# One decoder step on one core: attention passes written out unit by unit, with two score buffers per head, 64-row score tiles and 64-column values

## What is computed

```
s = einsum('nbqhgd,nbkhd->nbhgqk', qb, k2) * SCALE + bias      # 128 queries by 256 keys, head size 64
m = max(s, -1);  e = exp(s - m);  den = sum(e, -1)
o = einsum('nbhgqk,nbkhd->nbqhgd', e / den, v2)
lse = m + log(den)                                            # used to weigh head groups or the sink
```

## Time and profile before

| | before |
|---|---|
| median of 3 runs | 3253.78 us (3252.25 to 3257.07) |
| profiled execution, its own time | 3262.15 us |
| its span in the profile | 3260.3 us |
| mean granted TensorE clock | 0.939 of full speed |
| PE busy | 2920.5 us, 90% of the span |
| DVE, ACT, POOL busy | 1284.9, 894.0, 817.0 us |

### The profile page before, as it was taken

How to read it: one execution, slowest core, us unless ns; L and a number is a source line. 1 busy time by engine, 2 the same in 40 slices (tenths; PEclk the granted TensorE clock), 3 DMA queues, 4 the chain that set the end, 5 groups by cost and what they waited for, 6 DMA issues and landing times. The chain is left out here.

```text
span 3260.3 us, 54005 instructions
## 1 busy us (share of the span) xinstructions
PE 2920.5 (90%) x20802; PEld 2648.9 (81%) x20802; DVE 1284.9 (39%) x1934; ACT 894.0 (27%) x1725; POOL 817.0 (25%) x834
## 2 busy tenths in 40 slices
PE   8999989646899999999999999989945887899998
PEld 7999988525899998999989898979832224899997
DVE  2222243575422224222243434443368774422223
ACT  2222123431322212222222423242334331322212
POOL 2221112162122211222102123112326652122210
PEclk9999999957999999999999999999966888999999
DMA  7776622002466563666523142314216775466651
GB/s 245 247 234 168 206 60 70 5 24 64 144 221 211 162 205 126 220 212 209 181 63 93 38 121 67 91 32 123 73 41 223 272 272 190 141 211 223 214 167 44
DMA packets 467039, 482.09 MB, mean 148 GB/s; under 512 B 61054, under 2 KB 440047, under 8 KB 462632
## 3 DMA queue, kind: packets, MB, share of 16 engines
q1 hardware_dynamic: 456880, 467.46, 43.9%
q0 software_dynamic: 6416, 12.20, 1.3%
q10 hardware_dynamic: 3616, 0.69, 0.1%
HBM read 466.46 MB, written 199.42 MB: 204 GB/s over the span
## 5 line engine op out<-in xcount | busy, mean ns | idle before, releaser
L779 PE MATMUL bank<-sb_xh,sb_wl 128*128 128x272 f32 x4416 | 957.6, 293 | 50.7 <-DVE sb_wl L1483 28.5
L783 PE MATMUL bank<-sb_xh,sb_wh 128*128 128x272 f32 x4416 | 945.0, 291 | 0.0
L781 PE MATMUL bank<-sb_xl,sb_wh 128*128 128x272 f32 x4416 | 942.1, 290 | 0.0
L1483 DVE TENSOR_TENSOR sb_wl<-sb_raw,sb_wh 128x1024 fp32r<-128x1024 f32 (+1 forms) x340 | 453.0, 1333 | 1001.7 <-ACT sb_wh L1219 992.8
L779 PEld LDWEIGHTS bank<-sb_xh,sb_wl 128*128 128x128 f32 x4416 | 711.9, 191 | 58.8 <-DVE sb_wl L1483 31.9
L781 PEld LDWEIGHTS bank<-sb_xl,sb_wh 128*128 128x128 f32 x4416 | 712.8, 191 | 0.7
L783 PEld LDWEIGHTS bank<-sb_xh,sb_wh 128*128 128x128 f32 x4416 | 707.8, 191 | 0.0
L1219 ACT CAST sb_wh<-sb_raw 128x1024 fp32r<-128x1024 f32 (+1 forms) x340 | 376.4, 1109 | 972.7 <-PE bank L783 941.9
L1912 POOL CAST sb_hh<-sb_h 128x544 f32 x88 | 130.1, 1479 | 756.2 <-DVE sb_h L1492 756.2
L779 PE MATMUL bank<-sb_hh,sb_wl 128*128 128x272 f32 x1408 | 311.7, 292 | 0.5 <-DVE sb_wl L1483 0.5
L783 PE MATMUL bank<-sb_hh,sb_wh 128*128 128x272 f32 x1408 | 304.4, 288 | 0.0
(11 more groups left out here) (244 smaller groups left out, 2749.6 us busy)
## 6 DMA issues: line engine op xcount, KB each, us to landing
out_state_b_s<-in_cache_b_kv SPq DMA_DIRECT2D x176, 704.0 KB, 6.3
sb_dkvb<-in_cache_b_kv SPq DMA_DIRECT2D x144, 512.0 KB, 5.6
sb_raw<-in_ffn_w_gate SPq DMA_DIRECT2D x88, 512.0 KB, 3.9
sb_raw<-in_ffn_w_up SPq DMA_DIRECT2D x88, 512.0 KB, 4.5
sb_raw<-in_ffn_w_down SPq DMA_DIRECT2D x64, 704.0 KB, 4.8
sb_raw<-in_attn_b_w_qkv SPq DMA_DIRECT2D x72, 512.0 KB, 3.7
out_state_b_s<-in_cache_b_kv SPq DMA_DIRECT2D x32, 1016.0 KB, 8.1
out_state_b_s<-in_cache_b_kv SPq DMA_DIRECT2D x44, 176.0 KB
```

The lines of the kernel that those rows point to most:

```text
L779: pe.matmul(acc(s, h), wl[slot][:, k, :], hi(k)[:, halves[h]], start=start and k == 0, stop=False)
L781: pe.matmul(acc(s, h), wh[slot][:, k, :], lo(k)[:, halves[h]], start=False, stop=False)
L783: last = pe.matmul(acc(s, h), wh[slot][:, k, :], hi(k)[:, halves[h]], start=False, stop=end)
L1483: dve.tensor_tensor(wl[j % 2][:, 0:ph.chunks, :], raw[j][:, 0:ph.chunks, :], v.bitcast(F32), ALU.subtract).then_inc(wl_rdy, 1)
```

## The change

`skewed` now writes all units of a pass out, in the order in which the loop ran them; no registers are left in the passes. `scores` takes the queries straight from `q`: each head multiplies its own 64 partitions (`tile_position=(hd * HD, 0)`, a row tile), into its own bank (0 or 1 for the first head, 6 or 7 for the second). `values` takes only the head's own 64 columns. `add_bias` reads the two banks with two instructions and writes the maximum into `md`; `exps` reads it there and writes its sums there. `stats`, the staging on POOL, its clearing (`clear_staging`) and the tiles `qs`, `nm`, `dn` are gone. Those who waited for `st_done` wait for `ex_done`.

```
-        def skewed(eng, n_pairs, stages):
...
-            with eng.Fori(1, n_pairs) as i:
-                for s_ in range(4):
-                    for fn, lag in stages:
-                        fn(i + (s_ - lag) // 4, (s_ - lag) % 4)
+        def skewed(ps, stages):
+            for s_ in range(ps.units + max(lag for _, lag in stages)):
                 for fn, lag in stages:
+                    if 0 <= s_ - lag < ps.units:
+                        fn(s_ - lag, (s_ - lag) // 4, (s_ - lag) % 4)
...
-                    pe.wait_ge(qs_rdy, i * 4 + (ps.u0 + blk + 1))
-                    pe.wait_ge(sm_done, i * 4 + (ps.u0 + blk + 1))
+                def scores(k, i, blk):
+                    pe.wait_ge(sm_done, ps.u0 + k + 1)
                     for hd in range(2):
+                        rows = slice(hd * HD, (hd + 1) * HD)
...
+                            mm = pe.matmul(bank[6 * hd + k % 2][:, c:c + n], R["q"][g][rows, i, blk * P:(blk + 1) * P],
+                                           R["k"][g][rows, kt_, keys], start=True, stop=True, tile_position=(hd * HD, 0))
...
-                            mm = pe.matmul(bank[2 + b][:, hd * P:(hd + 1) * P], R["kt"][b][:, c:c + P], src,
+                            own = slice(vt * P + hd * HD, vt * P + (hd + 1) * HD)
...
+                            mm = pe.matmul(bank[2 + k % 2][:, hd * HD:(hd + 1) * HD], R["kt"][k % 2][:, c:c + P], src,
...
+                        last = act.activation(x, x, ACT.Exp, bias=md[:, blk, 0, c:c + 1], accum_out=md[:, blk, 1, c:c + 1])
...
-                    dve.scalar_tensor_tensor(x, s, SCALE, R["bias"][:, bass.ds(i * 2, 2), c0:256], ALU.mult, ALU.add).then_inc(sm_done, 1)
+                    for hd in range(2):
+                        last = dve.scalar_tensor_tensor(x[:, hd], bank[6 * hd + k % 2][:, c0:256], SCALE,
+                                                        R["bias"][:, 2 * i + hd, c0:256], ALU.mult, ALU.add)
...
-                skewed(dve, ps.pairs, [(add_bias, 0), (stats, 1), (output, 3)])
+                skewed(ps, [(add_bias, 0), (output, 3)])
...
-            def attention(ps, rn):
...
-                skewed(pool, ps.pairs, [(stage, 0)])
```

More of the change, by code:

```diff
@@ L988, in values @@
                         for kb in kbs:
[L989 to L992, removed]
+                            own = slice(vt * P + hd * HD, vt * P + (hd + 1) * HD)
+                            src = R["v"][kb][:, blk, own] if ps.dilated else R["v"][0][:, blk - 1 + kb, own]
                             c = hd * 256 + kb * P
-                            mm = pe.matmul(bank[2 + b][:, hd * P:(hd + 1) * P], R["kt"][b][:, c:c + P], src,
+                            mm = pe.matmul(bank[2 + k % 2][:, hd * HD:(hd + 1) * HD], R["kt"][k % 2][:, c:c + P], src,
                                            start=kb == kbs[0], stop=kb == kbs[-1])
                     mm.then_inc(pv_done, 1)
-                skewed(pe, ps.pairs, [(scores, 0), (turn, 1), (values, 2)])
+                skewed(ps, [(scores, 0), (turn, 1), (values, 2)])
                 end = ps.u0 + ps.units
@@ L1617, in output @@
[L1617 to L1628, removed]
@@ L1631, in step, with output @@
+                def output(k, i, blk):
+                    dve.wait_ge(pv_done, ps.u0 + k + 3)
+                    dve.tensor_copy(R["o"][ps.slot][:, blk, i * P:(i + 1) * P], bank[2 + k % 2][:, 0:P]).then_inc(oev_done, 1)
+                skewed(ps, [(add_bias, 0), (output, 3)])
             def step(ins):
@@ L1660, in group_weights @@
                 ps = pass_b[2 * r + 1]
-                dve.wait_ge(st_done, ps.u0 + ps.units)
+                dve.wait_ge(ex_done, ps.u0 + ps.units)
                 dve.wait_ge(oev_done, ps.u0 + ps.units + 2)
@@ L1855, in _ @@
                         dve.wait_ge(sink_rdy, 1)
-                        dve.wait_ge(st_done, pass_a.units)
+                        dve.wait_ge(ex_done, pass_a.units)
                         dve.wait_ge(oev_done, pass_a.units + 2)
@@ L1955, in run @@
                 store_out(r, r.n - 1)
[L1957 to L1964, removed]
-            def attention(ps, rn):
[L1967 to L1976, removed]
-                            last = pool.tensor_copy(R["qs"][b][rows, 2 * g + hd, :], src)
-                    last.then_inc(qs_rdy, 1)
-                skewed(pool, ps.pairs, [(stage, 0)])
             def exchange(ps):
                 r = (ps.n - 1) // 2
-                pool.wait_ge(st_done, ps.u0 + ps.units)
+                pool.wait_ge(ex_done, ps.u0 + ps.units)
                 pat = "(u c) e -> u c e" if ps.dilated else "(c u) e -> u c e"
@@ L2043, in _ @@
                     n_norm += 1
-                    if ph.kind == "down" and ph.f == 0:
-                        clear_staging(ph.l)
                     if ph.next:
@@ L2050, in _ @@
                     if ph is qkv[0]:
-                        attention(pass_a, ph.run)
                         decode(0)
@@ L2054, in _ @@
                         r, y = ph.run.rnd, int(ph.run.items[0][1] > 0)
-                        attention(pass_b[2 * r + y], ph.run)
                         exchange(pass_b[2 * r + y])
```

85 lines of the change are left out of this document (33 added, 52 removed).

## The result

| | before | after |
|---|---|---|
| median of 16 runs each | 3256.98 us (3249.88 to 3261.75) | 3271.21 us (3257.85 to 3294.62) |
| profiled execution, its span | 3262.15, 3260.3 us | 3273.63, 3271.8 us |
| mean granted TensorE clock | 0.939 | 0.917 |

The ratio is 1.0045, with an interval of 1.0031 to 1.0058. The kernel became 0.45% slower; I had forecast 1% faster. The 16 runs also scatter over 37 us, where the 16 of before scatter over 12. They stand almost in the order of their granted clocks: the fastest (3257.85 us) had 0.924, the slowest (3294.62 us) 0.907.

A forecast was written before the change was run, and what follows sets the result against it. The attention passes were taken as bound by a loop through PE and the other engines' answers. Loops -12.3 and -6.4, starts -12.0 sum to -30.7 us: 3231.5 profiled, 3223 as a median; range 3205 to 3257.

The forecast's parts named there:

- rival C: In the passes, PE is less busy and the clock falls to 1.2 GHz: +13.4 us, 3267 us; chance 0.12.
- Scores as row tiles: In the score products, both heads' row tiles run fully in parallel, so scores fall from 1.03 to 0.61 us.
- Rival A: In the scores, the two heads' row tiles don't overlap: loops lose 20.5 us, median 3244 us; chance 0.14.
- Changing between tile sizes: Between values and scores on PE, each change costs 0.20 us; one per loop charged, bounds 0 and 0.40.
- Rival D: Tile-size changes cost twice as much, the one before the turn not hidden: +9.6 us, 3233 us; within the forecast's 0.55.
- Values of 64 columns: In the value passes, each still needs its 0.11 us weight load, so no gain; bounds 0 or 0.055 us per pass.
- Rival B: 64-column value passes do gain, 0.055 us each, if loads go faster: 17.6 us, 3205 us; chance 0.10.
- Register work: In the pass loops, delays before values (596.10 to 596.40) and before DVE's bias (0.23 us, elsewhere 0.03) go when written out.
- DVE: Bias in two instructions takes 0.79 us for 0.73, +0.06; the dropped copies of `stats` count nothing.
- Starts: At the start of four passes, scores begin 2.4, 2.4, 3.6 and 3.6 us earlier: -12.0 us.
- The loops together: Four units take 9.38 us for 10.15, -12.3 us in all; dilated 9.88 for 10.68, -6.4 us.

## Why the prediction was wrong

**The step that failed** is rival C, the falling clock, in its price and in its chance. The forecast itself kept the clock at full (the prediction's "PE clock 1.00 after the first units").

The price was too low because C said "values stay at their loads" at half clock, 0.11 us each. I took that from transposes. They stream 32 columns, and their loads have 128 weight columns, as the value products' have, but only 32 rows; they follow one another in 0.11 us. The value products' loads, of 128 rows, take 0.21 at the same clock. Whether the rows make the difference, or that one is a transpose and the other an fp32 product, no run here tells. So the values double too. A dilated unit then has sixteen passes' time of 0.213 on PE (eight value passes, four turns, four pairs of score passes), 3.4 us, and some 0.4 for two changes of tile size: 3.81, as measured, with PE the bound. The prediction had a loop through the other engines there, at 2.92.

The chance of 0.12 was too low because I asked whether PE's busy share would be high enough (65 to 75% forecast, beside a stretch with 72% at full clock). The forecast of the share missed: it was 84% in the first pass and 96% in the third. And the share didn't tell: 96% at a clock of 0.54 after, 95% at 0.91 before (44.57 of 47.15).

**The sum closes on this.** The 169 us at half clock hold 112.5 us of dilated units, 112.5 / 3.81 = 30 units at a loss of 3.81 - 2.47 = 1.34, so 40 us. The other 57 hold 17 units at 3.37 (13.49 / 4) for 2.32, so 18 us (2.47 is 4.94 / 2, 2.32 is 9.29 / 4). Together they make 58 us, and the passes with full clock throughout are 294.9 - 238.1 = 56.8 us shorter. The 16 timed runs of the changed kernel agree. Between the fastest and the slowest, the mean clocks of 0.924 and 0.907 make 117 us more at half clock and 36.8 us more time, 0.31 us for each; the units' losses are 1.34 / 3.81 = 0.35 and 1.05 / 3.37 = 0.31.

By C's own prices (2.92 and 2.81) the same units would have lost 30 x 0.45 + 17 x 0.49 = 22 us, less than the 30.7 of the gains. So even with half clock in more than half of the pass time my C would have stayed on the fast side; that it "decides for slower once seven tenths of the passes run at 1.2 GHz" was wrong by the same term. C's 3267 lies near the measured 3271 by luck: it had every unit at half clock, at a third to a half of the true loss.

The other steps, in their order:

- *Scores as row tiles*: right. The heads start 0.01 us apart, and a second set of scores costs 0.43 us per loop, not 0.86. Rival A falls.
- *Changing between tile sizes*, 0.20 us: right. The first scores start 0.21 us after the last value pass's start, 0.10 more than a pass takes, and the group of four then lasts 0.70 us for the 0.61 forecast, 0.09 more. The Trainium skill says that a change of tiling mode drains the engine (TensorEngine Tiling (Array Packing), Key Properties). The trace agrees, with 0.10 + 0.09 us. Rival D falls with the loops of 4.39 and 4.90 us.
- *Values of 64 columns, no gain*: nearly right at full clock. The passes of the kernels with dummies are 2.6 us shorter with 64 (238.1 to 240.7), and in the kernel before 64 columns changed nothing (1.0006). Rival B, 17.6 us, falls. That they cost nothing was what went wrong.
- *Register work*: about right in the steady loops. In the forecast differences it comes to 0.45 us per four units (0.77 less 0.32 for the other terms), and 0.44 in dilated passes (0.80 less 0.36), 10.7 us in all. The loops written out gave 0.43 and 0.38, 9.9 us. The 14 us of the expectation counted 0.45 for every dilated loop, twice what the sum had.
- *DVE*, +0.06: right. The pair of bias instructions takes 0.76 us for 0.69.
- *Starts*: 11.1 of 12.0 us.
- *The loops together*: 9.29 us for 10.15 and 9.88 for 10.68 make 20.2 us at full clock, for 18.7 forecast.

With the dummies, the changed kernel stands at 3224.16 for the 3223 forecast, 29.5 us below the median of the kernel before on the same chip (26 by the ratio), for 30.7. That close a match is part luck: the dummies also do away with the half clock at each pass's start, 26 us of it in the kernel before, which the forecast didn't count. The fairer test is the kernel with 128-column values, which starts its passes at half clock as before: 27.7 us faster by its ratio (23 to 32). The terms at full clock were about right; the condition under all of them, that the clock stays as it was, was not.

What stays open: what the clock answers to, and how much of either edit a pass bears. Each alone is harmless, both together are not, and 128-column values or doubled scores mend it; nothing between was tried. Open, too, is where the 64-column kernel with dummies lost its clock in the slower ones of its runs. The other 9.6 us gained outside the passes are unexplained (7.5 of them lie after the last pass); the kernel before varies by 12 us from run to run.

## What to carry to other kernels

Before an edit that makes TensorE's work thinner, look where the clock is low at the start of such a stretch, and price the stretch with every PE term at half clock, weight loads included. Where PE came to bound that loop, as in the dilated passes here, the clock stayed at half to the pass's end; and the busy share in a profile didn't warn, since it was 95% with the clock coming back and 96% without. Work in a wait that nobody needs PE for (a dozen dummy products at the start of a pass) was worth 41 us to the changed kernel. Passes wider than needed cost 2.6 us in the five passes at full clock and, without any dummies, gave back 42.

## What the runs showed of the hardware

- The value product's weight load (128 rows, 128 columns, fp32) takes 191 ns at full and 334 ns at half clock on average; from one to the next it is 0.11 and 0.21 us. The load of a transpose with 32 rows and 128 columns follows the one before it in 0.11 us at half clock.
- Two row tiles of 64 rows run side by side, 0.01 us apart at the start, into different banks, although the kernel issues one head's product after the other's. Both heads in one bank weren't tried.
- The granted clock stayed at 0.50 through 56.4 us in which PE's records are full (56.34 us). The Trainium skill (TensorE: Matmul & The Clock Gate, Part 1) says that activity releases the throttle. Here PE's full records went with 0.54 over the pass, and the same pass with every score product twice with 0.96.
- Once granted, the full clock was held by the very work that didn't bring it back: a dilated pass took 41.6 us at 1.00 in the profiled execution with dummies, for 61.2 at 0.54.
